# RWKV scan of a hybrid diffusion step: quadrants crossed for every second pair of heads, inverse in 32x32 blocks, and VectorE work reordered

## The reference, cut to what matters

```python
def rwkv7_recurrence(r, decay, kk, b, k, v, s0):
    def step(s, inp):
        r_t, w_t, kk_t, b_t, k_t, v_t = inp
        sa = jnp.einsum('dbhvk,dbhk->dbhv', s, kk_t)
        s = s * w_t[..., None, :] - sa[..., :, None] * b_t[..., None, :] + v_t[..., :, None] * k_t[..., None, :]
        return s, jnp.einsum('dbhvk,dbhk->dbhv', s, r_t)
```

## Time and profile before

| | us |
|---|---|
| median of 3 runs (lowest, highest) | 2692.78 (2691.29, 2697.26) |
| the profiled execution | 2691.81 |
| its span, first to last instruction | 2689.8 |
| the RWKV scan's third turn | 67.81 |

### The profile page before, as it was taken

One profiled execution on the slowest core, in us unless ns is written; L12 is line 12 of the kernel. 1 busy time (PEld: TensorE's weight loads), 2 busy tenths in 40 slices (PEclk: granted clock), 3 DMA queues, 4 the chain that ended last, 5 costly groups with the idle time before them and its releaser, 6 DMA issues.

```text
span 2689.8 us, 74227 instructions
## 1 busy us (share of the span) xinstructions
PE 2448.0 (91%) x34058; PEld 1706.7 (63%) x34058; DVE 601.4 (22%) x1164; ACT 536.0 (20%) x1037; POOL 217.9 (8%) x243
## 2 busy tenths in 40 slices
PE   5899985999999769999999899998794999999998
PEld 3555564999994466777666345457453777766654
DVE  1113456666652330000000010106315000000001
ACT  3111043444421310000000036114413000000000
POOL 2000020333300010000000000003001000000000
PEclk8999997999999889999999999999896999999999
DMA  7665300000012269999999311110014999999970
GB/s 282 191 216 180 132 1 14 4 4 4 4 44 68 108 248 373 397 397 396 396 394 392 115 50 47 48 63 32 16 58 159 353 392 397 396 394 394 396 274 39
DMA packets 173468, 529.19 MB, mean 197 GB/s; under 512 B 23124, under 2 KB 27888, under 8 KB 173296
## 3 DMA queue, kind: packets, MB, share of 16 engines
q1 hardware_dynamic: 158688, 489.45, 48.1%
q10 hardware_dynamic: 10336, 24.21, 3.1%
q0 software_dynamic: 4272, 12.91, 1.4%
HBM read 506.75 MB, written 11.40 MB: 193 GB/s over the span
## 4 chain that ended last, share of the span: by engine, by line
PE 68%; issue 16%; DMA 5%; DVE 3%; ACT 2%; POOLq 1%; ACTq 1%; DVEq 1%; POOL 1%; SPq 0%
PE ps L1710 19%; PE ps L1725 17%; PE ps L1124 7%; PE ps L458 4%; PE ps L1840 4%; DMA big<-w_exp_down 3%; PE ps L1209 2%; PE ps L1912 2%; PE ps L1134 2%; PE ps L1908 2%; PE ps L460 1%; PE ps L830 1%; PE ps L438 1%; PE ps L1703 1%; PE ps L1196 1%
## 5 line engine op out<-in xcount | busy, mean ns | idle before, releaser
L1710 PE MATMUL ps<-rs,ring 128*64 128x80 f32 x12288 | 441.8, 233 | 5.8 <-issue 5.5
L1710 PEld LDWEIGHTS ps<-rs,ring 128*64 128x64 f32 x12288 | 429.9, 137 | 23.9 <-issue 23.0
L1811 DVE TENSOR_TENSOR big<-big,ps 128x320 f32<-128x320 f32 x64 | 28.3, 483 | 993.8 <-PE ps L1725 954.8
L1725 PE MATMUL ps<-big 128*80 128x512 f32 x512 | 226.4, 595 | 1.9 <-DMA big<-w_exp_down 1.5
L1725 PE MATMUL ps<-ring,big 128*80 128x512 f32 x512 | 225.0, 592 | 2.4 <-DVE big L1811 2.4
L555 PE MATMUL ps<-hT,ring 128*128 128x512 f32 x336 | 176.1, 606 | 11.1 <-ACTq L602 11.1
L1124 PE MATMUL ps<-big 64*64 64x64 f32 x5440 | 166.5, 219 | 16.9 <-DVEq L1095 16.9
L1781 ACT COPY big<-ps 80x512 f32<-80x512 f32 x64 | 34.1, 582 | 711.0 <-PE ps L1725 711.0
L1124 PEld LDWEIGHTS ps<-big 64*64 64x64 f32 x5440 | 163.1, 136 | 18.2 <-DVEq L1095 17.2
L1725 PEld LDWEIGHTS ps<-ring,big 128*80 128x80 f32 x512 | 76.6, 150 | 145.9 <-issue 141.8
L1725 PEld LDWEIGHTS ps<-big 128*80 128x80 f32 x512 | 74.3, 150 | 131.5 <-issue 129.8
(11 more groups left out here) (392 smaller groups left out, 3002.1 us busy)
## 6 DMA issues: line engine op xcount, KB each, us to landing
ring<-w_exp_up SPq DMA_DIRECT2D x124, 1024.0 KB, 10.8
ring<-w_exp_gate SPq DMA_DIRECT2D x68, 1024.0 KB, 12.1
big<-w_exp_down SPq DMA_DIRECT2D x64, 1024.0 KB, 11.3
ring<-w_exp_down SPq DMA_DIRECT2D x64, 1024.0 KB, 11.5
big<-w_exp_gate SPq DMA_DIRECT2D x60, 1024.0 KB, 10.6
big<-w_ada SPq DMA_DIRECT2D x22, 2048.0 KB, 8.7
ring<-w_in_odd SPq DMA_DIRECT2D x6, 2048.0 KB, 8.9
big<-big ACTq DMA_DIRECT2D x32, 256.0 KB, 6.4
```

The costliest lines, as they stand in the source:

```text
L1710: last = nc.tensor.matmul(ps[2 * m + j // 4][a:a + HALF, (j % 4) * SLOTS:(j % 4 + 1) * SLOTS], ex_blocks[ex_slot(q)][:, k % 2, j * P + a:j ...
L1725: last = nc.tensor.matmul(ps[4 + f][0:SLOTS, :], hid[:, k, :], ex_blocks[ex_slot(q)][:, k % 2, f * W:(f + 1) * W], start=(k == 0), stop=(k ...
```

## The change

The scan's mathematics stays. Five things change.

- **Halves exchanged.** For every second pair of heads (f = 1) a product's output goes to the other half of the partitions, in a second bank. Four matmuls in a row (f, g) thus use four different quadrants of the array. From there on, the token-side operands are in a new order of blocks, and copies and masks read two banks at once (`spread`, `placed`). Outputs cross back (`added_across`). The start and final states are turned head by head, and the chunk scales are crossed by 4 small matmuls and 4 small copies a turn (`place_em_pe`, `place_em_act`).
- **32x32 blocks.** Levels 0 to 4 treat the two diagonal 32x32 blocks of L alone: `pair_quarters` makes only these blocks and the corner between them, `quarters` does 32 matmuls of 32x32x32 on the four diagonal tiles in place of a call of 16, and T1, X, XT, Lm are half as wide. The last level handles the corner (`corner_left`, `corner_right`) and builds the full `XTf`.
- **R turned.** R is crossed into H's tile (one more product group and ScalarE copy for each direction).
- **VectorE's order.** The first masks (level 0) come ahead of everything else in a turn; R of this turn is made after X of level 0, not at the end of the turn before; the chunk scales and `Sc` come after Tk.
- **Waits.** The first pairs wait for the state read out (`sc_made`) and the crossed scales (`em_placed`); A's turn waits for `rwkv_y_kept`; K A waits for X.

Cut to its core:

```diff
+def place_em_pe(turn, pe):
+    for e in BOTH:
+        pe.wait_ge(sem("exps"), turn * 2 + (e + 1))
...
+        for g in range(2):
+            last = nc.tensor.matmul(ps[4 * e + 1][HALVES[1 - g], 0:4].rearrange("p (a u) -> p a u", a=2), half_ident[HALVES[g], :],
+                                    odd_pairs[HALVES[g]], start=True, stop=True)
+def quarters(b, lhs, rhs):
+    for j in range(RB):
+        for g in QUARTERS:
+            last = nc.tensor.matmul(ps[b][g, narrow(j)], lhs[g, j, :], quarter_ident[g, :] if rhs is None else rhs[g, j, :], start=True, stop=True)
+def pair_quarters(e):
+    for k in range(4):
+        for f in range(2):
+            j = 4 * (k // 2) + 2 * f + k % 2
+            for g in range(2):
+                for q in range(2):
+                    nc.tensor.matmul(ps[4 * e + f][QUARTERS[2 * (g ^ f) + q], narrow(k)], Bst[e][HALVES[g], j, QUARTERS[q]],
+                                     Ast[e][HALVES[g], j, QUARTERS[q]], start=True, stop=True)
...
+def corner_right(e):
+    for j in range(RB):
+        for h in range(2):
+            g = QUARTERS[2 * h + 1 - e]
+            nc.tensor.matmul(ps[4 * e + 3][QUARTERS[2 * h + e], narrow(j)], T1[e][g, j, :], XT[e][g, j, :], start=True, stop=True)
+            last = nc.tensor.matmul(ps[4 * e + 3][g, narrow(j)], quarter_ident[g, :], XT[e][g, j, :], start=True, stop=True)
+def across(b, lhs, rhs, apart=1):
+    for k in range(4):
+        for f in range(2):
+            for g in range(2):
+                last = nc.tensor.matmul(ps[b + apart * f][HALVES[g ^ f], k * N:(k + 1) * N], half_ident[HALVES[g], :] if lhs is None else lhs[f][k][HALVES[g]],
+                                        half_ident[HALVES[g], :] if rhs is None else rhs[f][k][HALVES[g]], start=True, stop=True)
 pe.wait_ge(sem("tile_ready"), n * 4 + 4)
 for e in BOTH:
-    each(4 * e + 1, Bst[e], Ast[e]).then_inc(sem("pairs_done"), 1)
-for e in BOTH:
-    turned(4 * e + 2, blocks_of(Ast[e])).then_inc(sem("abk_turned"), 1)
+    if n:
+        pe.wait_ge(sem("sc_made"), n * 4 + (e - 1))
+    pe.wait_ge(sem("em_placed"), n * 2 + (e + 1))
+    pair_quarters(e).then_inc(sem("pairs_done"), 1)
 for e in BOTH:
     pe.wait_ge(sem("rwkv_y_kept"), n * 2 + (e + 1))
-    each(4 * e, Kst[e], Ast[e]).then_inc(sem("pairs_done"), 1)
...
+    across(4 * e + 2, a_of[e], None).then_inc(sem("abk_turned"), 1)
...
-    turned(4 * e + 1, blocks_of(Lm[e])).then_inc(sem("x_product"), 1)
+    quarters(4 * e + 1, Lm[e], None).then_inc(sem("x_product"), 1)
...
+    pe.wait_ge(sem("x_updated"), n * 2 * (LEVELS - 1) + (e + 1))
+    across(4 * e, k_of[e], a_of[e]).then_inc(sem("pairs_done"), 1)
...
+    pe.wait_ge(sem("v_kept"), n * 2 + (e + 1))
+    across(4 * e + 2, None, r_of[e]).then_inc(sem("r_turned"), 1)
...
-        each(4 * e + 1, Lm[e], X[e]).then_inc(sem("lx_done"), 1)
+            quarters(4 * e + 1, Lm[e], X[e]).then_inc(sem("lx_done"), 1)
+        else:
+            corner_left(e).then_inc(sem("lx_done"), 1)
...
-            each(4 * e + 2, XT[e], T1[e]).then_inc(sem("x_product"), 1)
+            quarters(4 * e + 2, XT[e], T1[e]).then_inc(sem("x_product"), 1)
...
-            each(4 * e + 3, T1[e], XT[e]).then_inc(sem("xt_product"), 1)
+            quarters(4 * e + 3, T1[e], XT[e]).then_inc(sem("xt_product"), 1)
...
-    each(4 * e, nWG[e][:, :, 0:N], Btok[e])
-    each(4 * e + 3, nWG[e][:, :, 0:N], TbT[e]).then_inc(sem("phi_done"), 1)
+    each(4 * e + 1, nWG[e][:, :, 0:N], Btok[e])
+    each(4 * e + 2, nWG[e][:, :, 0:N], TbT[e]).then_inc(sem("phi_done"), 1)
...
+    if step and n + 1 < NT:
+        place_em_pe(n + 1, pe)
...
-            last = added(4 * e + 3, j, [(Vtok[e][:, j], TkT[e][:, j]), (nWG[e][:, j, N:P], TbT[e][:, j]), (state[e][:, c], Hm[e][:, j])])
+            last = added_across(4 * e + 2, k, [(two(Vtok[e], k), two(TkT[e], k)), (two(nWG[e][:, :, N:P], k), two(TbT[e], k)),
+                                               ([state[e][:, 2 * f + a] for f in range(2)], two(Hm[e], k))])
```

VectorE's order:

```diff
-for e in BOTH:
-    nc.vector.tensor_copy(em_now[e], em[e])
...
-    nc.vector.tensor_tensor(Sc[e], S[e], bc(em_kept[e], [P, RC, N], 2), ALU.mult)
 for e in BOTH:
     dve.wait_ge(sem("lt_kept"), n * 2 + (e + 1))
     mask_level(e, 0)
...
 for e in BOTH:
+    dve.wait_ge(sem("x_product"), n * 2 * (LEVELS - 1) + (e + 1))
+    nc.vector.tensor_tensor(X[e], narrow_eye, narrow_bank(4 * e + 1), ALU.subtract).then_inc(sem("x_updated"), 1)
+    mask_level(e, 1)
+if n:
+    for e in BOTH:
+        prepare_r_dve(n, e, dve)
+for e in BOTH:
     dve.wait_ge(sem("pairs_done"), n * 8 + (e + 3))
...
+for e in BOTH:
+    dve.wait_ge(sem("em_placed"), n * 2 + (e + 1))
+    nc.vector.tensor_copy(em_now[e], em_placed[e])
...
-for e in BOTH * more:
-    prepare_r_dve(n + 1, e, dve)
```

More of the change, by code:

```diff
@@ L48 @@
                       ("rot", P), ("cos", TS), ("sin", TS), ("edges", 2 * P),
-                      ("chain", 512), ("strict", 2 * N), ("within", 2 * N), ("level", 2 * LEVELS * N),
+                      ("chain", 512), ("strict", 2 * N), ("within", 2 * N), ("level", 2 * (LEVELS - 1) * QN), ("quarter_ident", QN), ("quarter", 2),
                       ("half_ident", N),
@@ L101, in constants @@
     lv = []
-    for h in [2 ** i for i in range(LEVELS)]:
+    s, tt = p[:, None] % QN, np.arange(QN)[None, :]
+    for h in [2 ** i for i in range(LEVELS - 1)]:
         same = s // (2 * h) == tt // (2 * h)
@@ L942, in build @@
         rwkvc = wr(ROWS0 - RWKV0)
-        chain, strict, within, level, half_ident = (const(n, rwkvc, RWKV0) for n in ("chain", "strict", "within", "level", "half_ident"))
+        chain, strict, within, level, half_ident, quarter_ident, quarter = (const(n, rwkvc, RWKV0) for n in (
+            "chain", "strict", "within", "level", "half_ident", "quarter_ident", "quarter"))
         ones_less_ka = wr(4)
         half, go_on = wr(RB), wr(1)
-        em, em_now = [wr(RB) for _ in BOTH], [wr(RB) for _ in BOTH]
+        em, em_placed, em_now = ([wr(RB) for _ in BOTH] for _ in range(3))
         em_kept, em_pair = [wr(RC) for _ in BOTH], [wr(RC) for _ in BOTH]
@@ L968, in build @@
         HALVES = (slice(0, N), slice(N, P))
+        QUARTERS = [slice(QN * g, QN * (g + 1)) for g in range(4)]
         def four(x):
@@ new lines, in pair_quarters @@
+                def pair_quarters(e):
[8 more added lines that the diff above has]
+                        for f in range(2):
+                            j = 4 * (k // 2) + 2 * f + k % 2
+                            for g in range(2):
+                                last = nc.tensor.matmul(ps[4 * e + f][QUARTERS[2 * (g ^ f) + e], narrow(k, 4 * QN)], Bst[e][HALVES[g], j, QUARTERS[e]],
+                                                        Ast[e][HALVES[g], j, QUARTERS[1 - e]], start=True, stop=True)
+                    return last
@@ new lines, in corner_left @@
+                def corner_left(e):
+                    for j in range(RB):
+                        for h in range(2):
+                            last = nc.tensor.matmul(ps[4 * e + 1][QUARTERS[2 * h + 1 - e], narrow(j)], corner[e][QUARTERS[2 * h + e], j, :],
+                                                    X[e][QUARTERS[2 * h + e], j, :], start=True, stop=True)
+                    return last
+                def corner_right(e):
+                    for j in range(RB):
+                        for h in range(2):
+                            g = QUARTERS[2 * h + 1 - e]
+                            nc.tensor.matmul(ps[4 * e + 3][QUARTERS[2 * h + e], narrow(j)], T1[e][g, j, :], XT[e][g, j, :], start=True, stop=True)
+                            last = nc.tensor.matmul(ps[4 * e + 3][g, narrow(j)], quarter_ident[g, :], XT[e][g, j, :], start=True, stop=True)
@@ L1210, in added, with added_across, two @@
                     return last
+                def added_across(b, k, terms):
+                    for t, (lhs, rhs) in enumerate(terms):
+                        for f in range(2):
+                            for g in range(2):
+                                last = nc.tensor.matmul(ps[b + f][HALVES[g ^ f], k * N:(k + 1) * N], lhs[f][HALVES[g]], rhs[f][HALVES[g]],
+                                                        start=(t == 0), stop=(t == 2))
+                    return last
+                def two(x, k):
+                    return [x[:, 4 * f + k] for f in range(2)]
                 for step in range(2):
@@ L1392, in rwkv_end_pe @@
                 for c in range(RC):
-                    last = nc.tensor.transpose(ps[4 + e][0:N, c * P:(c + 1) * P], S[e][:, c, :], ident)
+                    q = 2 * (c % 2) + c // 2
+                    for h in range(2):
+                        last = nc.tensor.matmul(ps[4 + e][0:N, c * P + h * N:c * P + (h + 1) * N], S[e][:, q, :],
+                                                ident[:, HALVES[h ^ (c % 2)]], start=True, stop=True)
             last.then_inc(sem("state_turned"), 1)
```

154 lines of the change are left out of this document (105 added, 49 removed).

## The result

The changed kernel takes 2837.86 us (median of 4 runs, 2833.28 to 2841.62) against 2692.03 (2689.13 to 2697.26) of the kernel before on the same chip: a ratio of 1.0539, 95% interval 1.0516 to 1.0561, 146 us slower. The profiled execution took 2833.28 us, its span is 2831.1. The forecast was 2613; the rival *TensorE is fed too slowly* had said 2824.

What follows compares the result with a forecast made beforehand. TensorE was taken to bound the scan (busy 67.79 of 67.81 us a turn). Four turns 15.9 us less (63.6), the last 16.8 less, 1 added: net 79.4, from 2691.81 to 2612.4, forecast 2613 as median; range 2592 to 2700.

Steps and rivals of the forecast that it cites:

- TensorE is fed too slowly: Rival, scan's new or across matmuls: pairs no faster than 27.3 ns, 54.6 ns a matmul, 2824 us; chance 0.20.
- pair of prices on TensorE: Scan matmuls: a quarter (32 columns, four tiles) costs 17.8 ns, one across (four quadrants) 31.3, against 58.4 now.
- point of decision: Feed rival, scan: faster than 35.3 ns a matmul, 17.7 ns a pair of records, the change gains.
- Its sign: Feed rival, in the inverse: 64 records of a quarter call would take 1.6 us or more.
- Quadrants don't overlap: Rival, matmuls across: row halves take turns, staying at 58.4 ns; 2646 us; 0.22 shared with clock and longer relays.
- loads bind: Rival, scan: only two tiles load at once, across costs 52 ns, a quarter 26; 2685 us; chance 0.08.
- The clock: Rival, scan: 1 us gaps partly lower TensorE's clock, some 5 us a turn, 2640; 0.22 shared with quadrants and relays.
- The rule of the Trainium skill: Scan matmuls: about 60 cycles overhead each, estimated 25 ns a record, sum about 100 us above the time before.
- The stages: Scan turn: stage one 14.0 us (18.67 now), levels 20.0 (30.40), W and G 3.9 (3.58), the rest 13.4 (15.16).
- VectorE's moved scales and R: Stage one: scales behind Tk cost nothing; R after X takes 1.3 us, TensorE idle about 1 us.
- new waits ahead of the pairs: Start of a scan turn: waits for state read and scales copied end no later than the relay, costed at nothing.
- the relays that were to bind at 51.9 us a turn: End of a turn: Phi and H kept, scan, centring, exponentials, B and K on GpSimd; 9.7 us after the change.

Runs made afterwards that it cites:

- resident loop: Kernel before plus three loops of extra 32x32x32 matmuls (bodies of 512, 1024, 4096 instructions; 8, 4, 2 passes), nothing left out: 2863.67 us.
- the loop in the kernel before: Kernel before with TensorE's levels 1 to 4 written as a loop of four passes, 384 instructions a pass: 2718.76 us, ratio 1.0097.
- old-order run: Changed kernel with VectorE's order of before (scales and scaled state ahead of first masks, R at end of previous turn): 2842.86 us, ratio 1.0565.
- wide kernel: Changed kernel with whole 64x64 inverse, A and R side by side (64x64x128), R made earlier, Tb's mask ahead of X: 2676.05 us, 0.9961 of kernel before.
- line of quarters: Kernel before plus 1024 matmuls of 32x32x32 in straight line ahead of the third turn, nothing left out: 2750.95 us.
- line of matmuls across: Kernel before plus 1024 matmuls of 64x64x64 on four quadrants, two banks, in straight line ahead of the third turn: 2756.89 us.

## Why the prediction was wrong

**The step that failed** is the pair of prices on TensorE, 17.8 ns for a quarter and 31.3 for a matmul across, taken as what they would cost in the kernel. As own paces they were near: in a resident loop a quarter takes 2 x 9.6 = 19.2 ns, and within a burst one across takes 2 x 14.6 = 29.2. What was missing is a floor under both, the feed: 29.2 ns a pair, 58.4 ns a matmul of either kind, over three times the one price and nearly twice the other. The upper ends that the prediction gave, 54.6 and 58.4 ns, were near what the kernel paid. At 29.2 ns the 3240 records of a turn take 94.6 us; the turn took 99.3, and the last 4.7 us are not accounted for piece by piece. The rival had the price at 27.3 ns a pair and came out 14 us under the measurement; its point of decision, 17.7 ns a pair, was passed by far. That its price came so near is partly luck: the streaming of that row by itself gives 108.5 / 4 = 27.1 ns. Its sign, 64 records of a quarter call in 1.6 us or more, appears only with the pause counted (half of 3.74 us is 1.87); within a burst 64 records take 0.7 or 1.0 us.

**Why it got only 0.20.** The prediction held against it that "at 27.3 and 29.2 ns the streaming alone explains the pace". For 29.2 that was true, as the loop in the kernel before showed. But a pace that streaming explains says nothing of how much faster instructions could come: the two limits happen to coincide at 64x64 on two quadrants. So did TensorE's 67.79 busy of 67.81 us, which I read as a bound that any saving lowers. A row that could have raised the question was at hand, the page's count of instruction blocks: 2152 records of a turn are 4304 instructions, 17 blocks in 67.8 us, and the densest row on which I leaned had 256 instructions in 40.57 - 37.08 = 3.49 us. Whether that row was streaming or the feed no run here tells.

**The other rivals.** *Quadrants don't overlap* falls (14.6 ns within a burst), and so does *loads bind*, which had across at 52 ns. *The clock* did fall, to a mean of 0.69 in the third turn and 0.59 in its levels, where TensorE was busy for 32.29 of 52.42 us. Bursts at either level start equally far apart, so between them the lower clock costs nothing that shows; in W and G, at a mean of 0.61, it is part of 6.71 us instead of 3.58. The rule of the Trainium skill (TensorEngine Tiling, Instruction Overhead), which gave an estimate of 25 ns a record and 100 us over the time before, was nearer in its sum than my forecast, but its mechanism is not what is seen: the same quarters start every 9.6 ns in a resident loop. The other rule of the Trainium skill (TensorEngine Tiling, Restrictions and Gotchas) is that different row tiles can't write one PSUM bank at a time. It is not borne out as a price: those quarters write one bank from four row tiles at 9.6 ns a pair, where 32 columns alone stream for 27.1.

**The remaining steps.** The stages were put at 14.0, 20.0, 3.9 and 13.4 us and took 26.06, 52.42, 6.71 and 14.13. Levels and pairs, where the small blocks are, missed most; the rest, with hardly more records than before (526 against 516), was nearly right. That VectorE's moved scales and R cost next to nothing is in line with the old-order run. The new waits ahead of the pairs were undone in no run; in the third turn TensorE's idle time ahead of the pairs is put down to issue. Of the relays that were to bind at 51.9 us a turn, the one through the state's scale behind the centring did bind, as forecast, but for 0.6 us a turn (L1504 above). In the wide kernel TensorE also waited 0.4 us for GpSimd's K at the start of the fourth turn (653.62 us), and in its third turn 0.2 us twice for ScalarE. Whether the relays would bind as forecast, with all instructions at hand, was not tried; a turn of 3247 records doesn't fit where 1536 instructions stay.

## What to carry to other kernels

Before splitting matmuls into smaller tiles, count the instruction blocks of the stretch: straight code of small f32 matmuls was fed here at 3.5 to 4.0 us a block, 27 to 31 ns for each load and matmul. Smaller tiles or more quadrants give nothing once that floor is reached, and more instructions then cost time whatever their size (levels: 934 records in 30.40 us before, 1764 in 52.42 after). What helped here is more streaming per instruction (the kernel with N of 128 on four quadrants was 0.4% faster than the one before), or a loop whose body stays resident: 84 us less in the changed kernel, but 26 us more in the kernel before, where its openings cost time and there was nothing to win. A busy share of 100% on an engine names a bound, not how far below it the next one lies.

## What was not expected of the hardware

- A block of 256 instructions is taken in 3.5 to 4.0 us, though a burst needs only 1.4 to 2.1 us of it. Why not faster, the trace does not say; the transfers of q8 have a share of 1.8% of the DMA engines in the changed kernel's third turn.
- TensorE can take a load and a matmul every 9.6 ns when the code is resident: four 32x32 tiles, 1536 pairs in 14.79 us.
- Loop bodies of 1536 instructions stay resident and bodies of 2048 don't; the jump back costs about 0.2 us (idle times of 0.16, 0.17 and 0.22 us ahead of a pass).
- Four quadrants of 64x64 through two banks give twice the pace of two, 14.6 against 29.2 ns a record.
- In the line of quarters, bursts of 1.93 us with pauses of 1.8, the granted clock was 0.50; in the line of matmuls across, bursts of 2.09 us with pauses of 1.6 to 1.9, it was 1.00. No run tells why.
